# Two norms joined between the blocks of a transformer, half a swa group half a unit on, and a table load moved

## The reference

```python
        mixed = jnp.concatenate([o_sb, o_mb, o_mem], axis=-1)
        x = x + jnp.einsum('btc,cd->btd', mixed, w_out[layer])
    return rms_norm(x, final_norm_g)
...
    h = jnp.concatenate([filler, meta, x], axis=1)          # 16 meta rows ahead of x
    u = rms_norm_2(h, pre_mix_gain[l])
    proj = u @ w_in[l]                                      # swa, diff, gates
    ...
    o_swa = windowed_gqa_sink_attention(qa, ka, va, ...)    # 16 query heads, 4 key heads
    o_diff = differential_attention(...)                    # 8 heads
    ...
    h = h + rms_norm_2(merged @ w_out[l], post_mix_gain[l])
    u = rms_norm_2(h, pre_ffn_gain[l])
    f = (silu(gate) * up) @ w_ffn_out[l]
    h = h + rms_norm_2(f, post_ffn_gain[l])
```

## Time and profile before

| | us |
|---|---|
| median of the 3 runs | 833.49 |
| lowest and highest | 832.29 and 833.73 |
| profiled execution | 831.91 |
| its span, from first to last instruction | 830.1 |
| TensorE busy in the span | 801.1 |
| granted clock of TensorE, mean | 0.995 of full |

### The profile page before, as it was taken

The page is one execution under the profiler, slowest core; times in us unless marked ns, Lnnn a source line. Parts: engine busy times, 40 slices in busy tenths (PEclk is TensorE's granted clock), DMA queues, the critical chain, the costliest instruction groups (busy, mean ns, idle before and its releaser), DMA issues.

```text
span 830.1 us, 12690 instructions
## 1 busy us (share of the span) xinstructions
PE 801.1 (97%) x4238; PEld 651.3 (78%) x4238; DVE 497.9 (60%) x731; ACT 467.8 (56%) x1004; POOL 136.5 (16%) x204
## 2 busy tenths in 40 slices
PE   7999999999999998899999999999999999999996
PEld 5887778887777885877778888778887888888885
DVE  5456565684566555666765767666787544555454
ACT  5677586475666555555566565654557433444352
POOL 2011021000243110434433546000000000000000
PEclk9999999999999999999999999999999999999999
DMA  8964553469764546442323435456775645465631
GB/s 237 285 174 145 151 169 104 144 190 286 228 203 128 190 152 197 138 123 85 89 77 96 128 116 164 128 178 228 244 230 160 203 151 179 153 203 191 209 133 51
DMA packets 147294, 137.78 MB, mean 166 GB/s; under 512 B 15024, under 2 KB 115648, under 8 KB 147232
## 3 DMA queue, kind: packets, MB, share of 16 engines
q1 hardware_dynamic: 145136, 129.89, 50.9%
q0 software_dynamic: 2096, 7.09, 3.1%
HBM read 135.90 MB, written 1.05 MB: 165 GB/s over the span
## 4 chain that ended last, share of the span: by engine, by line
PE 82%; ACT 5%; DVE 5%; POOL 4%; issue 3%; DMA 1%; DVEq 0%; SPq 0%; ACTq 0%; POOLq 0%
PE psum L1182 66%; PE psum L1160 7%; PE psum L1281 3%; PE psum L1416 3%; ACT w_hi L1463 2%; ACT probs L1590 1%; POOL rtmp L1128 1%; POOL rtmp L1130 1%; DVE w_lo L1659 1%; DVE probs L1802 1%; PE psum L1202 1%; POOL rtmp L1132 1%; PE psum L1342 1%; POOL stage L1134 1%; PE psum L1384 1%
## 5 line engine op out<-in xcount | busy, mean ns | idle before, releaser
L1659 DVE TENSOR_TENSOR w_lo<-raw,w_hi 128x1024 fp32r<-128x1024 f32 (+1 forms) x234 | 274.1, 1194 | 118.8 <-ACT w_hi L1463 83.4
L1182 PE MATMUL psum<-w_hi,h_hi 128*128 128x512 f32 (+1 forms) x656 | 259.9, 396 | 4.8 <-DVE w_lo L1659 2.2
L1463 ACT ACTIVATE w_hi<-raw 128x1024 fp32r<-128x1024 f32 (+1 forms) x234 | 230.9, 1011 | 41.0 <-PE psum L1182 17.2
L1182 PE MATMUL psum<-w_lo,h_hi 128*128 128x512 f32 (+1 forms) x656 | 247.2, 377 | 0.0
L1182 PE MATMUL psum<-w_hi,h_lo 128*128 128x512 f32 (+1 forms) x656 | 246.6, 376 | 0.0
L1182 PEld LDWEIGHTS psum<-w_hi,h_hi 128*128 128x128 f32 x656 | 124.1, 189 | 31.4 <-issue 14.8
L1182 PEld LDWEIGHTS psum<-w_lo,h_hi 128*128 128x128 f32 x656 | 123.9, 189 | 19.2
L1182 PEld LDWEIGHTS psum<-w_hi,h_lo 128*128 128x128 f32 x656 | 124.3, 190 | 15.4
L1182 PE MATMUL psum<-w_hi,m_hi 128*128 128x512 f32 x152 | 60.3, 397 | 1.2 <-DVE m_lo L1717 1.2
L1182 PE MATMUL psum<-w_lo,m_hi 128*128 128x512 f32 x152 | 59.3, 390 | 0.0
L1182 PE MATMUL psum<-w_hi,m_lo 128*128 128x512 f32 x152 | 59.2, 389 | 0.0
(11 more groups left out here) (171 smaller groups left out, 1001.1 us busy)
## 6 DMA issues: line engine op xcount, KB each, us to landing
raw<-in_w_in SPq DMA_DIRECT2D x112, 256.0 KB, 3.8
raw<-in_w_ffn_in SPq DMA_DIRECT2D x88, 256.0 KB, 4.1
raw<-in_w_in SPq DMA_DIRECT2D x24, 512.0 KB, 3.9
raw<-in_w_out SPq DMA_DIRECT2D x24, 512.0 KB, 3.5
raw<-in_w_in SPq DMA_DIRECT2D x64, 192.0 KB, 2.7
raw<-in_w_ffn_out SPq DMA_DIRECT2D x22, 512.0 KB, 4.2
meta_w<-in_w_in SPq DMA_DIRECT2D x10, 1024.0 KB, 7.9
raw<-in_w_mem_kv SPq DMA_DIRECT2D x8, 512.0 KB, 3.9
```

The lines of the kernel that those rows point to most:

```text
L1182: last = nc.tensor.matmul(psum[:, bank, 0:n], sx[name][:, c, t * P:(t + 1) * P], wx[:, kk, 0:n], start=u["first"] and kk == 0 and z == 0, ...
L1463: nc.scalar.activation(weights(u)[0][:, :, 0:n], raw[:, u["raw"], :, 0:n], ACT.Copy)\
L1659: nc.vector.tensor_tensor(lo[:, :, 0:n], raw[:, u["raw"], :, 0:n], hi[:, :, 0:n].bitcast(F32), ALU.subtract)\
```

## The change

It has four parts.

1. *Joined norms* (`row_scale`, `row_sum`, `twin`). With x the rows before the final norm, g its gain and r its factor, the second norm's mean of squares is r² · mean((x·g)²). Both factors together are 1 / sqrt(mean((x·g)²) + eps · mean(x²) + eps²). So VectorE makes xn = x·g in halves of 512 columns as soon as the half is added (`row_scale`), ScalarE sums the squares of x and of x·g by halves (`row_sum`, 8 in all), GpSimd makes the bias eps·(X0 + X1) + eps² + Y0 with three operations on 128x1 for each tile, ScalarE takes Ln and Exp, and VectorE multiplies xn by that and by the second gain, again by halves. The final norm's x itself is made behind the units of kv = 3, by the old steps without the squares.
2. *Order at the border.* The splits of units 81 and 82 come ahead of the additions; meta group 4 comes in two halves between the two halves of the turns; tile 1's turns come behind all four `unit_a` of kv = 0 instead of behind three; the additions of meta groups 3 and 4 come apart, in kv = 0 and kv = 1. Each half of `meta_w` is loaded when the matmuls of that half of the group before are done, and waited for alone, and META_LOAD of group 4 is 3 instead of 4.
3. *SLOTS for kv = 0* of its own: the second pair's scores, soft, scale, turn_p, turn_tm, out_t and mix_t come 0.5 later. The row that was there stays for kv = 1 to 3.
4. *Tail.* The table load and the split of unit 233 come behind the last `turn_f`.

The core of the diff:

```diff
-META_LOAD = (2, 2, 2, -4, 4)
+META_LOAD = (2, 2, 2, -4, 3)
...
     "swa": dict(turn_qk=(3.25, 2.75), scores=(4.45, 4.45, 6.45, 6.45), soft=(4.95, 4.95, 6.95, 6.95),
                 scale=(5.95, 7.95), turn_p=(6.5, 6.5, 8.5, 8.5), turn_tm=(6.9, 8.9), out_t=(7.5, 9.5),
                 mix_t=(7.95, 9.95)),
+    "swa0": dict(turn_qk=(3.25, 2.75), scores=(4.45, 4.45, 6.95, 6.95), soft=(4.95, 4.95, 7.45, 7.45),
+                 scale=(5.95, 8.45), turn_p=(6.5, 6.5, 9, 9), turn_tm=(6.9, 9.4), out_t=(7.5, 10),
+                 mix_t=(7.95, 10.45)),
...
-            final, after = norm(source="x", dest="x"), norm(source="x", dest="xn")
-            line.append(final[0])
-            line.extend(("unit_b", u) for u in (a[3], b[3]))
-
+            final, after = norm(source="x", dest="x", twin=True), norm("twin", source="x", dest="xn")
             metas.append(meta_group(4))
             metas[4]["evac_later"] = True
-            line.extend([after[0], ("meta", metas[4]), final[1]])
-            line.extend(norm_turns("xn", "h", 0))
-            line.append(after[1])
+            for us, g in ((a, outs[0]), (b, outs[1])):
+                line.extend([("unit_a", us[3]), row_scale(final, g, 0), row_sum(final, g, 0, "x"),
+                             row_sum(final, g, 0, "y")])
+            line.append(("hold", "begun"))
+            turns = norm_turns("xn", "h", 0)
+            line.extend([("unit_b", a[3]), row_scale(final, outs[0], 1), after[0], row_sum(final, outs[0], 1, "x")])
+            line.extend([("unit_b", b[3]), ("meta", metas[4], (0, KC // 2)), turns[0]])
+            line.extend([row_sum(final, outs[0], 1, "y"), row_scale(final, outs[1], 1)])
+            line.extend([("meta", metas[4], (KC // 2, KC)), ("hold", None), ("splits", "one"), ("hold", "begun"), turns[1]])
+            line.extend([row_sum(final, outs[1], 1, "x"), row_sum(final, outs[1], 1, "y"), after[1]])
+            line.append(("ahead", SPLIT_AHEAD))
...
         if kv == 0:
-            line.extend(("unit_a", u) for u in g["units"][:3])
-            line.extend(norm_turns("xn", "h", 1))
-            line.append(("unit_a", g["units"][3]))
-            line.extend(("evac", dict(g=metas[n], t=0)) for n in (3, 4))
-            line.extend(("unit_b", u) for u in g["units"])
+            us = g["units"]
+            us[3]["evac_later"] = True
+            line.extend(("unit_a", u) for u in us)
+            line.extend(norm_turns("xn", "h", 1) + [("evac", dict(g=g, t=0)), ("hold", None), ("splits", "one")])
+            line.extend([("unit_b", us[0]), ("unit_b", us[1]), ("evac", dict(g=metas[3], t=0))])
+            line.extend([("unit_b", us[2]), ("unit_b", us[3])])
+        elif kv == 1:
+            add(g)
+            line.insert(-2, ("evac", dict(g=metas[4], t=0)))
+        elif kv == 3:
+            add(g)
+            line.extend(final)
...
-    line.append(("tables", None))
     held = outs_of(nf - 3) + outs_of(nf - 2)
-    line.extend(("unit_a", u) for u in held[:3])
-    line.append(("turn_f", dict(j=nf - 1, f=last_g)))
-    line.append(("unit_a", held[3]))
+    line.extend(("unit_a", u) for u in held[:2])
+    line.extend([("hold", "begun"), ("unit_a", held[2]), ("turn_f", dict(j=nf - 1, f=last_g))])
+    line.extend([("hold", None), ("splits", "one"), ("tables", None), ("unit_a", held[3])])
...
+                if what == "twin":
+                    pool.wait_ge(row_summed, 4 * t + 3)
+                    link(nc.gpsimd.tensor_tensor(bias, X0, X1, ALU.add))
+                    link(nc.gpsimd.tensor_scalar(bias, bias, EPS, EPS * EPS, ALU.mult, ALU.add))
+                    nc.gpsimd.tensor_tensor(bias, bias, Y0, ALU.add).then_inc(row_bias, 1)
...
+                elif what == "twin":
+                    act.wait_ge(row_bias, t + 1)
+                    act.wait_ge(row_summed, 4 * t + 4)
+                    link(nc.scalar.activation(rs, Y1, ACT.Ln, bias=twins[:, t:t + 1]))
+                    nc.scalar.activation(rs, rs, ACT.Exp, scale=-0.5).then_inc(rstd_ready, 1)
...
+                elif what == "row_scale":
+                    nc.vector.tensor_tensor(xn[:, t, at], x[:, t, at], gain[:, gain_use[i][0], at], ALU.mult)\
+                        .then_inc(row_scaled, 1)
```

More of the change, by code:

```diff
@@ L196, in lay_out @@
     free, user = deque(range(NSLOT)), {}
-    for what, arg in timeline:
+    for what, arg, *_ in timeline:
         if what == "more_slots":
@@ L229, in part @@
             splits()
-        if u["last"] and (g["by"] or g["kind"] == "gates"):
+        if u["last"] and (g["by"] or g["kind"] == "gates") and (tile or "evac_later" not in u):
             steps.append(("evac", dict(g=g, t=tile)))
@@ L241, in part @@
             splits()
-    for what, arg in timeline:
+    for what, arg, *rows in timeline:
         if what == "splits":
-            splits(split + 1 if arg == "one" else arg)
+            splits({None: len(order), "one": split + 1}.get(arg, arg))
         elif what == "hold":
@@ L259, in lay_out @@
         elif what == "meta":
-            steps.append((what, dict(g=arg, chunks=(0, KC))))
+            steps.append((what, dict(g=arg, chunks=rows[0] if rows else (0, KC))))
             if not arg.get("evac_later"):
@@ L424, in number @@
             s["half"] = pl.next("halves")
-        elif what in ("norm", "addnorm", "metanorm"):
+        elif what == "row_scale":
+            s["ready"] = ("evac_dve", g["free"][s["t"]])
+            scales_of[(g["n"], s["t"])] = pl.next("row_scales")
+        elif what == "row_sum":
+            s["ready"] = ("evac_dve", g["free"][s["t"]])
+            s["outs"] = pl.count["outs"]
+            s["sum"] = pl.next("row_sums")
+            if s["of"] == "y":
+                s["scaled"] = scales_of[(g["n"], s["t"])]
+        elif what in ("norm", "addnorm", "metanorm", "twin"):
             N, t = s["norm"], s["t"]
@@ L587, in make_plan @@
             metas.append(meta_group(3))
+            line.append(("ahead", SPLIT_AHEAD + 2))
             line.append(("flush", dict(g=metas[3])))
+            line.append(("splits", None))
         else:
@@ L901, in build @@
         for i, (what, s) in enumerate(STEPS):
-            if what in ("norm", "metanorm", "addnorm", "half") and "gain" in s["norm"]:
+            if what in ("norm", "metanorm", "addnorm", "half", "twin", "row_scale") and "gain" in s["norm"]:
                 gain_use[i] = s["norm"]["gain"]
@@ L905, in build @@
                 continue
-            if what in ("norm", "metanorm", "half") or (what == "evac" and s["g"]["kind"] == "gates"
+            if what in ("norm", "metanorm", "half", "twin", "row_scale") or (what == "evac" and s["g"]["kind"] == "gates"
                                                           and s["g"]["n"] % 2 == 0 and s["t"] == 0):
@@ L1693, in _ @@
                                                    in1=x[:, t, :], op0=ALU.mult, op1=ALU.add).then_inc(norm_done, 1)
+                elif what == "row_scale":
+                    t, n = s["t"], s["g"]["n"]
+                    at = slice(n * 512, (n + 1) * 512)
+                    dve.wait_ge(*gain_use[i][1:])
+                    wait(dve, s["ready"])
+                    nc.vector.tensor_tensor(xn[:, t, at], x[:, t, at], gain[:, gain_use[i][0], at], ALU.mult)\
+                        .then_inc(row_scaled, 1)
+                elif what == "twin":
+                    N, t = s["norm"], s["t"]
+                    dve.wait_ge(*gain_use[i][1:])
+                    dve.wait_ge(rstd_ready, s["rstd"])
+                    c = 4 * (N["n"] % 4) + 2 * t
+                    for n in range(2):
+                        at = slice(n * 512, (n + 1) * 512)
+                        nc.vector.scalar_tensor_tensor(out=xn[:, t, at], in0=xn[:, t, at], scalar=nstat[:, 16 + c:17 + c],
+                                                       in1=gain[:, gain_use[i][0], at], op0=ALU.mult, op1=ALU.mult)\
+                            .then_inc(norm_done, 1)
                 elif what in ("norm", "metanorm"):
```

76 lines of the change are left out of this document (63 added, 13 removed).

## The result

The changed kernel takes 839.35 us (median of 7 runs, 836.34 to 841.44), the kernel before 833.48 us (7 runs, 831.58 to 834.03). The ratio on record is 1.0079, with a 95% interval of 1.0067 to 1.0092: the changed kernel is slower. The two medians lie 5.9 us apart (a quotient of 1.0070). For the changed kernel 832.2 us was forecast. Its runs go with TensorE's mean granted clock: 836.34 us at 0.997, 841.44 us at 0.988. The profiled execution, 841.16 us with a span of 839.3 and a clock of 0.988, is one of the long ones, 9.2 us above the span of before.

What follows compares the result with a forecast made beforehand. TensorE, at work 801.1 of 830.1 us, was taken as the bound. Terms −4.1 − 1.0 + 3.1 + 1.8 − 1.05 = −1.25 us gave 830.7 profiled, 832.2 against the median, range 829.0 to 835.3.

Steps and rivals of the forecast that it cites:

- the prediction's own sign of being wrong: Whole kernel: the prediction is wrong if TensorE's total idle time ends outside 26 to 31 us.
- the shift: First swa group, second pair half a unit later: longer TensorE waits, a loss of +3.1 us.
- the postponed final norm: Behind kv = 3: VectorE's 2 x 1.28 us ahead of a reduction cost +1.8 us (0.8 to 2.6).
- Joined norms at the border: Border between the blocks: joined norms and new order start swa work earlier, −4.1 us (3.1 to 5.0 gained).
- The rotary wait: Behind the border: TensorE's 1.13 us wait for GpSimd's rotary work shrinks by 1.0 us, 0.3 if two w_lo meet it.
- if scaling slips behind a split: First swa group: upper end of the second pair's cost, +4.6 us instead of +3.1.
- rival 1: First swa group: turns come 1 us sooner, +1.0 instead of +3.1, total 830.1 before the added difference; chance 0.26.
- The first wait: First swa group: TensorE waits 2.94 us, 362.62 to 365.56, for the first pair's scaled probabilities, where it waited 1.42.
- the copies' wait: First swa group, second pair: ScalarE's p_t copies come behind the next exponentials, so TensorE waits 2.4 us.
- of the 2.56 us some 0.8 come back: Final norm behind kv = 3: the small operation after the reduction runs once rotary work is done, regaining 0.8 us.
- The tail: End of kernel: later table load and split remove most of the 1.21 us m_lo wait, −1.05 us (−0.7 to −1.15).
- rival 2: First swa group: waits bring TensorE's lower clock; one drop with +4.6 gives 835.2 us, two 836.7; chance 0.16.

Runs made afterwards that it cites:

- b_tail: Kernel before with only the tail part (table load and split of unit 233 behind the last turns): 830.36 us, ratio 0.9988.
- b_shift: Kernel before with only the first swa group's second pair half a unit later (row swa0 of SLOTS): 839.29 us, ratio 1.0087.
- b_meta: Kernel before with meta weights' halves loaded and waited for apart and META_LOAD 3 for group 4, norms as before: 832.42 us, ratio 0.9999.
- a_slots: Changed kernel with the old places of the first swa group's second pair: 832.59 us, ratio 1.0009.
- a_fill2: Changed kernel with 13, 5, 9, 9 and 3 idle constant matmuls at five TensorE waits, ending about within them; swa results disturbed: 835.65 us, ratio 1.0051.
- a_both: Changed kernel with old SLOTS; final norm behind tile 1's joined norm (tile 0) and behind tile 1's second unit (tile 1): 833.21 us, ratio 1.0015.
- a_best: Changed kernel with old SLOTS; final norm behind tile 1's joined norm (tile 0) and at the end of kv = 1 (tile 1): 829.69 us, ratio 0.9973.
- a_best2: Like a_best, but tile 1's final norm one unit earlier, ahead of the last unit of kv = 1: 827.15 us, ratio 0.9945.
- a_fill: Changed kernel with 20, 9, 14, 5 and 15 idle constant matmuls at five places where TensorE waits; swa results disturbed: 840.08 us, ratio 1.0101.

## Why the prediction was wrong

The time, 839.35 us, lies above the range of 829.0 to 835.3, and the prediction's own sign of being wrong came up: TensorE's idle time is 33.7 us, outside 26 to 31. The mechanisms named were nearly all there. What failed in the sum are three terms: the shift (+3.1, measured +4.65), the postponed final norm (+1.8, measured +3.0, or +3.6 by its own waits) and the slow clock in the swa groups, which the sum had at nothing (measured +5.5 us of busy time in the profiled execution). The border's gain was 1.0 us too large as well. The waits alone, +4.7 us, bring the kernel to 838.2 us, outside the range already; the fastest runs of the two kernels, 831.58 and 836.34 us, also lie 4.8 us apart.

- **Joined norms at the border**: −4.1 forecast, of 3.1 to 5.0; measured −3.07 at the unit that starts at 341.87. The first swa matmul came at 330.91 for 330.2, and the uncovered h_lo of tile 1 took 1.32 us for 0.9. Of the first 0.7 us, 0.5 are the third GpSimd operation's below, which Ln waits for. A slip of the working cost nothing: the second half of x·g was put at 325.1, but x is there at 324.9 by the earlier trace rows, and 0.69 more gives 325.6, where it came (325.56). The last sum still ended at 326.41, ahead of GpSimd's 327.00. The meta weights' wait went and the clock stayed up, as said. GpSimd's operations took 0.20, 0.19 and 0.69 us for the first tile, and 0.2, 0.19 and 0.19 us for the second tile:

```profile
325.75 0.20 POOL L1125 TENSOR_TENSOR eps_col<-hsum 128x1 f32<-128x1 f32 x1 [25.51 <-ACT p_t L1553]
326.04 0.19 POOL L1126 TENSOR_SCALAR eps_col<-eps_col 128x1 f32<-128x1 f32 x1
326.31 0.69 POOL L1127 TENSOR_TENSOR eps_col<-eps_col,hsum 128x1 f32<-128x1 f32 x1
...
326.26 0.69 DVE L1792 TENSOR_TENSOR xn<-x,gain 128x512 f32<-128x512 f32 x1
...
333.00 0.19 POOL L1127 TENSOR_TENSOR eps_col<-eps_col,hsum 128x1 f32<-128x1 f32 x1
```

  VectorE's row_scale ran from 326.26 to 326.95, and the third operation ended only behind it, at 327.00. The Trainium skill's rule on the shared port (SBUF — State Buffer, section Who interferes with whom) agrees with the two rows at 326.3.
- **The rotary wait**: −1.0 forecast, −0.75 measured. It was 1.13 us in the one execution before, but 1.78, 1.74 and 1.78 in b_tail, b_shift and b_meta, which have the old border, and 0.38 or 0.39 after and in a_slots, so the gain is 0.75 to 1.4 us by which execution is taken.
- **The shift**: +3.1 forecast, with +4.6 as the upper end "if scaling slips behind a split". It slipped. (For a chain 1 us shorter the prediction has +1.5 here and +1.0 in rival 1, which do not agree; the sum used neither.) The first wait was 3.22 us for the forecast 2.94, the copies' wait 2.22 for 2.4. The one I had at nothing is the 1.46 us ahead of the second pair's turned probabilities. Three rows on the way to it, of ScalarE and VectorE:

```profile
372.83 0.86 ACT L1522 ACTIVATE w_hi<-raw 128x768 fp32r<-128x768 f32 x1
...
373.77 1.23 DVE L1751 TENSOR_TENSOR w_lo<-raw,w_hi 128x768 fp32r<-128x768 f32 x1 [0.36 <-ACT w_hi L1522]
...
375.65 1.36 DVE L1912 TENSOR_TENSOR probs<-probs,rec 128x1088 f32<-128x1088 f32 x1
```

  The exponentials were done by then, but VectorE's scaling stands behind w_lo of the next unit in the order, which waits for w_hi, which ScalarE does behind the exponentials and mix_hi. All waits of that stretch come to 6.9 us after, against 2.2 before, the vanished 0.58 of the earlier trace rows among them as in the forecast: +4.65, the upper end. The failed step is that the sum took the second pair's chain without the splits that stand in it, and kept them for the upper end alone.
- **The postponed final norm**: +1.8 forecast, +3.0 of waits measured in the table's row; since the vanished 0.58 us stands in that row and is counted with the shift here, the norm's own waits come to 3.6 us. The failed step is "of the 2.56 us some 0.8 come back". VectorE's and GpSimd's rows say why:

```profile
398.77 3.09 DVE L1816 SCALAR_TENSOR_TENSOR x<-x,nstat,gain 128x1024 f32<-128x1024 f32 x2
401.78 1.28 DVE L1878 TENSOR_REDUCE stats<-psum 128x4 f32<-128x1088 f32 x1
...
403.68 0.84 DVE L1884 TENSOR_TENSOR stats<-stats,sinks 128x4 f32<-128x4 f32 x1
...
398.97 1.81 POOL L1190 TENSOR_TENSOR stage<-rtmp 128x320 f32<-128x320 f32 x1
```

  The two steps took 3.09 us instead of 2.56 beside the rotary work, and were held up together with it: one of its operations took 1.81 us where 0.87 is usual. So the rotary work was not over when the small operations came, and the second one still took 0.84 us. Nothing came back, and a bank that is free 0.91 us late and 0.78 us at the fourth group come on top.
- **The tail**: −1.05 forecast, −0.9 measured.
- **The clock**: this was rival 2, with a chance of 0.16 and one or two drops, and it is what happened in the profiled execution, three times. I held against it that 2.94 us stand between units without a gap. The rows show that this doesn't protect: the clock was down by 362.00, after one wait of 3.22 us, and for the 10 us ahead of it (348.66 to 358.71) the trace lists no wait of TensorE's. It was down again at 410 us after 0.91 and 2.21 us. The Trainium skill (TensorE: Matmul & The Clock Gate, section HAM oscillation — how this bites in real kernels) tells of a kernel whose bursts of matmuls start at the slow level each time, behind waits for DMA of some 3 to 5 us. The drop behind 3.22 us agrees with that; those behind 1.46 and 2.22 us, and 0.91 and 2.21 us, came behind shorter waits than the page's. The sum had the clock at +0 there. By these rows a drop costs 1.6 us (two for the +3.2 of the first group) to 2.3 us, and b_tail shows that a group of waits need not bring one, so the sum should have carried a share of such a price for each of the waits of 2 to 3 us that it forecast itself.

Of waits alone, by the table's rows and with the border's as 2.5 after against 4.3, the terms give −1.8 − 0.75 + 5.2 + 3.0 − 0.9 = +4.75 us, against 33.7 − 29.0 = 4.7 in the trace. The busy time gives the other 4.5: the slow clock's three stretches (+5.5) against the one of before (−1.1). In the median run the clock's part must be smaller: the medians differ by 5.9 us, 1.2 us more than the waits, and a_fill2 puts it at some 2.3 us.

## What to carry to other kernels

A step that is moved to make room has to be walked along every engine's order at the new place, with the splits, copies and loads that stand ahead of it there. Two experiments in which one tile's final norm stands a unit apart differ by 2.5 us. Where a gap of TensorE's is made longer or a second one is put near it, count a share of the slow clock behind it as part of its price. And a change in four parts is to be measured part by part: here three parts gain 4.6 us together, once the final norm stands right, and one row of a table cost more than all of that.

## What the runs showed of the hardware

TensorE's clock fell to about 0.5 after a wait of 3.22 us, after 1.46 and 2.22 us with 2.1 us of work between, and after 0.91 and 2.21 us with 1.5 us between; each time 3 to 5.5 us of matmuls followed at or near that level. In other runs it fell behind single waits of 4.80 us (a_both), 2.52 us (a_best) and 1.74 us (b_shift), and it stayed at 1.00 behind 1.81 us (b_shift), 1.78 us (b_tail) and, in b_tail, behind the border's 2.05, 0.98 and 1.25 us, which brought it down in the kernel before. So no length of a wait alone decided it. In the changed kernel the runs' spread goes with the clock: 836.34 to 841.44 us at 0.997 to 0.988. In a_best2, whose longest wait in the swa groups is 0.57 us, the runs lie between 827.11 and 827.40 us, though their mean clocks read 0.995 to 0.999; a difference of 0.004 in that figure shows in no time there.

Twenty 128x128 fp32 matmuls of constants filled 4.5 us (a_fill), 0.22 us each, where the profile's eight transposes of the same shape take 1.06 us. VectorE's 128x1024 step with two SBUF inputs and GpSimd's 128x320 one overlapped and both took longer, 1.55 us (half of 3.09) for 1.28 and 1.81 us for 0.87. A load that GpSimd had to start held its own later work for as long as the load's buffer was in use (7.08 us in a_both). Operations on 128x1 took 0.19 to 0.20 us on GpSimd where VectorE did not meet them, and 0.20 to 0.30 us on ScalarE.
